# A decoder step on one core: unused products in front, a halved first transfer, and several moves in the order of work

## The chip, the cores and the metric

The kernel runs on one core of a Trainium2 chip. The metric is the device time of one execution in microseconds (us). A core has five engines with queues of their own: PE (matrix products and transposes, written to PSUM), DVE and ACT (vector and scalar work), POOL (here small copies, and the queue that issues some transfers) and SP (issues the other transfers). Sixteen DMA engines serve all queues.

## The reference, cut to what matters

One layer of a decoder works on 256 prompt rows and on 64 sample rows (8 sequences of 8 tokens, each with 1024 past positions in 8 pages). The rows are normed and go through one input projection:

```python
xn = rmsnorm(x, norm_mix)
proj = jnp.einsum('btd,dc->btc', xn, w_in)            # 1024 x 4888
# mixer A: compressed, selected and window attention, mixed by gates;
# the compression: hid = gelu(blocks @ w1), comp = hid @ w2
# mixer B: differential attention with its own keys and values
y_nsa  = jnp.einsum('btf,fd->btd', o_nsa.reshape(b, t, Q_NSA_W), w_br_nsa)
y_diff = jnp.einsum('btf,fd->btd', o_diff.reshape(b, t, V_DIFF_W), w_br_diff)
x = x + jnp.einsum('btd,de->bte', gate_nsa * y_nsa + gate_diff * y_diff, w_out)
h = rmsnorm(x, norm_ffn)
x = x + moe_ffn(h, ...)    # top 4 of 32 experts, each 1024 x 2048 and 1024 x 1024
```

`gate_nsa` and `gate_diff` are the sigmoids of the projection's last 2048 columns. Past keys and values come from paged caches by a page table.

## The kernel before

Everything is float32. Each engine's order is written out by hand, with semaphores between engines; a queue waits in order, so what stands behind a waiting instruction waits too. A product of float32 shows as two records of PE, and 512 columns are its widest.

**The head.** SP issues small constants, the three row tiles (`TILE_ORDER` is sample, prompt 0, prompt 1), then the chunks of `w_in`, 2 MB each, in slots of `wslot`. PE transposes each tile in two halves (`tp`, L2134). ACT evacuates the first half of a tile (L2386) and DVE the second (L2503), into `xnT`. ACT takes the squares for the norm (`square_of`, L2376), that of the first tile between two evacuations. Then `pe_projection` (L355 for prompt rows, L364 for sample rows) goes through chunks 0 to 5 in pairs; each product is 128 rows of `w_in` by 512 columns, 8 of them (`k`) for a row tile and a chunk.

**Transposes, gates, compression.** `qk_groups` are 15 groups of transposes. With the first eight PE does one of the 8 products of gate unit 0 each (`gate_products`, L2158); with the others four steps of the compression's first layer (`hidden`, L2170, 45 columns each). The twelve gate units fill PE between the stages of prompt attention: stage `s` is scores (L2212), gate units of `GATE_FIRST[s]`, transposed weights of the stage before, values. Scores of a stage wait for `e_ready`, the exponentials of the stage before (ACT, L2447).

**Turns.** Sample attention is done in 4 turns of two sequences. PE transposes pages of keys (`kd0` to `kd7` and `nk0` to `nk7`), selected keys (`sel`), window keys (`win`) and weights (`pd`, `ps`, `pw`, `pm`), in the order of `LOOP_GROUPS`; `l_tp` counts the groups. POOL's queue carries the pages for compression (`cmp_pages`, L469) and the differential values (`values_in`, L525); SP's carries the differential keys and the selected pages. DVE turns the compression pages of the next turn (L840) in its own order, ahead of evacuations of this turn; `dif_values` (L666) waits for the pages of `values_in`. In the last turn PE also does the branch products of the first output part (`branch_products(pe, 0, half)`, L1146), which wait for the semaphore `br`.

**Merge.** `sync_merge` is SP's queue from there: branch weights (`br_n`, `br_d`), the gates' stored values, `w_out`, small tensors and biases, and the experts' weights. PE's part is `pe_merge`: branch products, transposes of merged rows (`merged_t`, L1305, each after DVE's `m_done`), output products (`out_proj`, L1326), router logits, ranks, and the first rows picked for the experts (`first_pick`, L1365). The expert weights that take the place of `w_out` are issued after `z_full` is 5, that is after the last output product:

```python
            sp.wait_ge(z_full, 5)
            for h in range(2):
                down_weights(sp, 0, 0, h)
            down_weights(sp, 1, 1, 0)
            for c in range(4):
                sp.wait_ge(e_used, c + 1)
                gate_up_weights(sp, 1, c)
```

**Experts.** 32 experts, each with four 2 MB transfers (L1162) and two more (L1165, the last expert's in smaller pieces), stream through fixed places; a place is filled again when PE has used it (`e_used`).

## Time and profile before

| | us |
|---|---|
| median of 3 runs | 1439.93 |
| the runs | 1437.8 to 1440.52 |
| profiled execution, its own time | 1438.28 |
| its span in the profile | 1436.6 |
| PE busy | 1383.1 (96%) |
| DVE, ACT, POOL busy | 467.6, 285.6, 98.3 |

The span is the part from the first to the last instruction; the execution's time is 1.68 us more. PE is busy nearly throughout, but a busy PE may be one whose next record waits for data: the chain of work that ended last has 73% on PE and 18% on DMA.

### The profile page before, as it was taken

To read this page: it belongs to the slowest core of one execution; us is meant where nothing else is said; L and a number is where in the kernel's file an instruction comes from. 1 tells how busy PE (TensorE), PEld (TensorE's weight loads), DVE (VectorE), ACT (ScalarE), POOL (GpSimd) and SP (SyncE) were. 2 spreads that over 40 slices of the span, in tenths; PEclk is the share of its full clock that TensorE was granted. 3 is DMA by queue.
4 is the path that set the end of the run, shared out by engine and by line. 5 is a ranking of instruction groups with operands and counts; after the bars stand their busy time and mean duration, and the time that the engine had idled before them with its cause. 6 is when DMAs were issued, how large, how long until landed. Compare 5 with 4: busy or idle time off the path is not lost.

```text
span 1436.6 us, 19580 instructions
## 1 busy us (share of the span) xinstructions
PE 1383.1 (96%) x7350; PEld 610.6 (43%) x7350; DVE 467.6 (33%) x1022; ACT 285.6 (20%) x609; POOL 98.3 (7%) x217
## 2 busy tenths in 40 slices
PE   7999999999989999999999999999999999999987
PEld 3446555777764453333333333333333333333322
DVE  1113465555636352222133133121331331222314
ACT  2003344445542210110111100100111111010102
POOL 1000120624310000000000000000000000000000
PEclk9999999999999999999999999999999999999999
DMA  7334674899887599999999999999999999999996
GB/s 269 117 117 159 242 194 130 294 328 310 318 286 237 228 421 426 428 430 427 428 430 428 427 429 429 427 429 430 427 428 430 429 427 428 430 427 429 430 427 252
DMA packets 75468, 509.39 MB, mean 355 GB/s; under 512 B 19066, under 2 KB 25698, under 8 KB 46082
## 3 DMA queue, kind: packets, MB, share of 16 engines
q1 hardware_dynamic: 61378, 477.88, 81.7%
q0 software_dynamic: 13184, 27.82, 6.0%
q10 hardware_dynamic: 864, 3.15, 0.6%
q8 instruction: 25, 0.41, 0.1%
q14 instruction: 17, 0.14, 0.0%
HBM read 502.29 MB, written 10.62 MB: 357 GB/s over the span
## 4 chain that ended last, share of the span: by engine, by line
PE 73%; DMA 18%; DVE 3%; issue 3%; SPq 1%; ACT 1%; POOLq 0%; POOL 0%; DVEq 0%; ACTq 0%
PE PS L1464 25%; PE PS L1494 11%; DMA arena<-in_w_gate_up 10%; PE PS L1438 6%; PE PS L355 6%; DMA arena<-in_w_down 5%; PE PS L2158 4%; PE PS L1430 4%; PE PS L604 3%; PE PS L590 3%; PE PS L1326 2%; PE PS L364 1%; SPq L254 1%; PE PS L1481 1%; DMA arena<-in_cache_diff_k 1%
## 5 line engine op out<-in xcount | busy, mean ns | idle before, releaser
L1464 PE MATMUL PS<-arena 128*64 128x512 f32 x2048 | 456.1, 595 | 13.9 <-DMA arena<-in_w_gate_up 12.9
L1464 PEld LDWEIGHTS PS<-arena 128*64 128x64 f32 x2048 | 141.5, 137 | 294.9 <-issue 263.2
L1494 PE MATMUL PS<-arena 128*64 128x512 f32 x1024 | 226.9, 594 | 2.3 <-DMA arena<-in_w_down 2.2
L1920 DVE TENSOR_SCALAR arena<-PS 128x512 f32<-128x512 f32 x32 | 22.1, 692 | 450.9 <-PE PS L1473 449.9
L1494 PEld LDWEIGHTS PS<-arena 128*64 128x64 f32 x1024 | 71.7, 137 | 150.5 <-issue 144.3
L1438 PE MATMUL PS<-arena 128*128 128x512 f32 (+1 forms) x180 | 84.2, 608 | 0.0
L1430 PE MATMUL PS<-arena 128*128 128x512 f32 (+1 forms) x192 | 79.4, 618 | 4.5 <-ACT arena L1630 3.7
L355 PE MATMUL PS<-arena 128*128 128x512 f32 (+1 forms) x192 | 79.5, 576 | 1.9 <-DMA arena<-in_w_in 1.9
L1287 POOL COPY arena<-arena 96x64 bf16 (+1 forms) x34 | 8.1, 240 | 988.2 <-PE PS L1501 942.9
L1841 DVE TENSOR_TENSOR arena<-PS,arena 128x512 f32<-128x512 f32 x32 | 21.8, 688 | 162.1 <-PE PS L1446 161.2
L1615 ACT ACTIVATE arena<-arena 128x512 f32<-128x512 f32 x32 | 20.2, 631 | 268.1 <-DVE arena L1920 268.1
L1622 ACT ACTIVATE arena<-PS 128x512 f32<-128x512 f32 x32 | 19.1, 597 | 250.7 <-PE PS L1481 250.7
L604 PE MATMUL PS<-arena 128*128 128x252 f32 x256 | 68.1, 382 | 0.0
L590 PE MATMUL PS<-arena 128*128 128x128 f32 (+1 forms) x456 | 65.8, 277 | 2.3 <-DMA arena<-in_cache_diff_k 1.5
L1629 ACT ACTIVATE arena<-PS 64x512 f32<-64x512 f32 x31 | 18.3, 591 | 226.3 <-PE PS L1501 226.3
L590 PEld LDWEIGHTS PS<-arena 128*128 128x128 f32 (+1 forms) x456 | 53.1, 141 | 17.0 <-issue 5.8
L2158 PE MATMUL PS<-arena 128*128 128x512 f32 x128 | 59.6, 608 | 0.6 <-ACT arena L2395 0.6
L858 ACT ACTIVATE arena<-PS 128x512 f32<-128x512 f32 (+5 forms) x96 | 44.6, 492 | 61.4 <-PE PS L590 59.4
L355 PEld LDWEIGHTS PS<-arena 128*128 128x128 f32 x192 | 37.2, 195 | 43.7 <-issue 42.3
L1438 PEld LDWEIGHTS PS<-arena 128*128 128x128 f32 (+1 forms) x180 | 31.6, 188 | 46.3 <-issue 46.3
L604 PEld LDWEIGHTS PS<-arena 128*128 128x128 f32 x256 | 42.7, 190 | 4.6 <-issue 1.5
L1430 PEld LDWEIGHTS PS<-arena 128*128 128x128 f32 (+1 forms) x192 | 24.9, 171 | 43.9 <-issue 36.9
(289 smaller groups left out, 1280.9 us busy)
## 6 DMA issues: line engine op xcount, KB each, us to landing
arena<-in_w_gate_up SPq DMA_DIRECT2D x128, 2048.0 KB, 20.1
arena<-in_w_down SPq DMA_DIRECT2D x62, 2048.0 KB, 22.1
arena<-in_w_in SPq DMA_DIRECT2D x9, 2048.0 KB, 12.9
arena<-in_cache_diff_k SPq DMA_DIRECT2D x64, 256.0 KB, 6.0
arena<-in_cache_diff_v POOLq DMA_DIRECT2D x64, 256.0 KB, 5.0
arena<-in_cache_cmp_kv POOLq DMA_DIRECT2D x64, 128.0 KB, 3.9
arena<-in_cache_sel_kv SPq DMA_DIRECT2D x64, 128.0 KB, 6.9
arena<-in_w_out SPq DMA_DIRECT2D x1, 4096.0 KB, 14.2
```

The source lines that it names most:

```text
L355: last = nc.tensor.matmul(bank(proj_bank(q, 2 * s + t))[:, 0:w], xnT[:, k, 128 * t:128 * t + 128], chunk_at(j)[:, k, 0:w], start=(k == 0), ...
L590: last = nc.tensor.transpose(place[0:c, col:col + r], src, ident[0:r, 0:r])
L604: last = nc.tensor.matmul(hidden_at[c], w1[:, c, l, :], cmp_window(c, l), start=(l == 0), stop=(l == CB // 2 - 1))
L858: copy = lambda d, s: nc.scalar.activation(d, s, ACT.Copy)
L1326: last = nc.tensor.matmul(bank(Z_BANK[v])[p:p + r], mT[:, k, 128 * t:128 * t + r], w_out[:, k, 512 * nh:512 * nh + 512], start=(k == 0), s ...
L1430: last = nc.tensor.matmul(out, spread[:, 128 * t:128 * t + ROWS[t]], ypair[:, 512 * h:512 * h + 512], start=True, stop=True)
L1438: last = nc.tensor.matmul(bank(h), pick[0:ROWS[t], t], hn[t][0:ROWS[t], 512 * h:512 * h + 512], start=(t == 0), stop=(t == 2))
L1464: last = nc.tensor.matmul(bank(2 + role + 2 * u)[64 * h:64 * h + 64], hTm[:, k, BS * u:BS * u + BS], gu_w[:, k, D * role + 512 * h:D * rol ...
L1494: last = nc.tensor.matmul(bank(6 + u)[64 * h:64 * h + 64], aT[u][:, c % 4, 64 * (c // 4):64 * (c // 4) + 64], down_w[u][c // 4][:, c % 4, ...
L1841: st(V.tensor_tensor(hTm[:, :, BS * u:BS * u + BS], x, gffn.unsqueeze(2).to_broadcast([128, KD, BS]), ALU.mult), x_out)
L1920: st(V.tensor_scalar(g1, bank(2 + 2 * u), LIM, None, ALU.min), g1_ready)
L2158: last = nc.tensor.matmul(bank(7), xnT[:, k, 128 * t:128 * t + 128], chunk_at(j)[:, k], start=(k == 0), stop=(k == KD - 1))
```

## The change

Eight edits, in the order of the program:

- DVE sets 128x512 elements to 1 (`warm`), and PE does products on them that nobody reads: 512, 512 and 256 columns wide ahead of the first transposes, 256 after each of the first two tiles, 512 after the third. ACT takes the first tile's square after all evacuations.
- The first chunk of `w_in` comes in two transfers of half the rows (`k` 0 to 3, 4 to 7), and PE waits for the second after four products.
- The first three products of gate unit 1 are done with transpose groups 11, 12 and 13, among the compression's products, instead of after the first scores.
- POOL issues the compression pages of turn 1 before the differential values of turn 0. In the last turn the second sequence's values are issued after `kd7` instead of after `pd2`.
- The branch weights have two semaphores (`br_n`, `br_d`), and those of mixer A come as whole 128-partition transfers, one for each `k`, instead of half the partitions for two `k`.
- The first gate values (1 MB) are loaded with the other two, after the last scores.
- `branch(1)` goes ahead of PE's wait for the last evacuations of the turns.
- In the router's part, rows of tile 2 are picked where those of tile 0 were, and the other way about.

```diff
             past(pool, l_tp, NPAGE + group_at("kd0") + 1)
+            cmp_pages(pool, pages_of(POOL, 1, 0), 1, 0)
             values_in(pages[0], 0, 0, True)
             for n in (10, 11):
                 gates_stored(pool, n)
             pool.wait_ge(stored, n_stored)
-            cmp_pages(pool, pages_of(POOL, 1, 0), 1, 0)
             values_in(pages[1], 0, 1, True)
...
-                past(pool, l_tp, i * L_TP + (NPAGE + group_at("pd2", last) + 1))
+                past(pool, l_tp, i * L_TP + (NPAGE + group_at("kd7" if last else "pd2", last) + 1))
                 values_in(pages[1], i, 1)
...
                 if final:
-                    arrived(pe, "br")
+                    arrived(pe, "br_n")
                     branch_products(pe, 0, 0)
                 l_out_done(pe, i, group_at("pm", final), final)
                 nsa_values()
                 if final:
+                    arrived(pe, "br_d")
                     branch_products(pe, 0, 1).then_inc(br_full, 1)
...
             for c in range(2):
                 sp.wait_ge(l_hid, 2 * PAIRS_OF_SEQ - 1 + c)
-                for g in range(2):
-                    load(sp, "br", br_n[64 * g:64 * g + 64, 2 * c:2 * c + 2], w_nsa[g, :, 2 * c:2 * c + 2])
+                for k in (2 * c, 2 * c + 1):
+                    load(sp, "br_n", br_n[:, k], w_nsa[k])
                 for k in (c, c + 2):
-                    load(sp, "br", br_d[:, k], w_dif[:, k])
-                if c == 0:
-                    for n in (10, 11):
-                        gates_stored(sp, n)
-                    past(sp, l_tp, NPAGE + (PAIRS_OF_SEQ - 1) * L_TP + group_at("kd7", True) + 1)
-                    load(sp, "gates0", gsig[0:ROWS[0], 0], gate_pre[0:ROWS[0], 0:2 * D])
+                    load(sp, "br_d", br_d[:, k], w_dif[:, k])
+            for n in (10, 11):
+                gates_stored(sp, n)
             past(sp, l_sc, PAIRS_OF_SEQ * SCORES)
-            for t in (1, 2):
+            for t in range(3):
...
+            branch(1)
             l_out_done(pe, PAIRS_OF_SEQ - 1, len(LAST_GROUPS) - 1, True)
-            branch(1)
             branch(2)
...
-            for j in range(2):
-                load_chunk(j)
+            load(sp, "w_first", chunk_at(0)[:, 0:KD // 2], w_in[:, 0:KD // 2, 0:CHUNKS[0][1]])
+            sp.dma_start(chunk_at(0)[:, KD // 2:], w_in[:, KD // 2:, 0:CHUNKS[0][1]]).then_inc(w_arrived[0], 16)
+            load_chunk(1)
...
+            def unused_products(widths):
+                for w in widths:
+                    nc.tensor.matmul(bank(7)[:, 0:w], warm[:, 0:128], warm[:, 0:w], start=True, stop=True)
+
+            pe.wait_ge(warm_ready, 1)
+            unused_products((512, 512, 256))
             for k, t in enumerate(TILE_ORDER):
...
+                unused_products((256,) if k < 2 else (512,))
...
                     hidden(range(4 * (n - QK_HID), 4 * (n - QK_HID) + 4))
+                    if n in GATE_AMONG:
+                        gate_products(1, range(GATE_AMONG.index(n), GATE_AMONG.index(n) + 1))
...
-                    gate_products(g, range(KD if s < n - 1 else KD // 2))
+                    gate_products(g, range(0 if s else len(GATE_AMONG), KD if s < n - 1 else KD // 2))
...
+            V.memset(warm, 1.0).then_inc(warm_ready, 1)
```

`GATE_AMONG` is (11, 12, 13). `first_pick(0, ...)` and `first_pick(2)` change places in `pe_merge`, and `square_of` of the first tile moves behind the loop over tiles.

## Rows read from the trace of the kernel before

**Rows 1.** The page's 40 slices: GB/s that the DMA engines moved.
```profile
GB/s 269 117 117 159 242 194 130 294 328 310 318 286 237 228 421 426 428 430 427 428 430 428 427 429 429 427 429 430 427 428 430 429 427 428 430 427 429 430 427 252
```

**Rows 2.** The chain that ended last: start us, us, what.
```profile
3.50 10.29 DMA arena<-in_w_in
...
262.14 11.80 DMA arena<-in_cache_cmp_kv
...
466.58 0.46 PE PS L1305 x4
...
1418.27 3.65 PE PS L1494 x16
```

**Rows 3.** Waits of SP's queue: us in total, times, longest.
```profile
SPq L1165 <- PE PS L1326: 30.6, 1, 30.6
```

**Rows 4.** Timeline of PE at the last output products: start us, us, operation.
```profile
500.06 1.12 PE L1326 MATMUL PS<-arena 128*128 128x512 f32 x2
```

**Rows 5.** Timeline of the head; in brackets the idle time before, and its releaser.
```profile
5.49 1.31 PE L2134 MATMUL PS<-arena 8*128 8x8 f32 x9 [5.49 <-DMA arena<-in_x_sample]
...
10.11 1.94 PE L2134 MATMUL PS<-arena 128*128 128x128 f32 x8 [0.47 <-ACT arena L2386]
...
12.08 0.69 DVE L2503 TENSOR_TENSOR arena<-PS,arena 128x512 f32<-128x512 f32 x1 [1.72 <-PE PS L2134]
...
13.93 26.35 PE L355 MATMUL PS<-arena 128*128 128x512 f32 x55 [1.88 <-DMA arena<-in_w_in]
...
18.33 0.34 PEld L355 LDWEIGHTS PS<-arena 128*128 128x128 f32 x1 [0.52 <-issue]
...
19.52 0.19 PEld L355 LDWEIGHTS PS<-arena 128*128 128x128 f32 x1 [0.24 <-issue]
```

**Rows 6.** Windows: us; PE, PEld, DVE, ACT, POOL busy; PE clock, DMA share, GB/s.
```profile
10.00:25.00 15.00, 13.01 (x28) 6.42 (x29) 2.04 (x9) 5.80 (x13) 0.00 (x0) 1.00 1.06 388
...
136.00:138.00 2.00, 2.00 (x12) 1.92 (x13) 0.18 (x1) 0.45 (x2) 0.00 (x0) 0.50 0.03 8
```

**Rows 7.** Timeline of PE around the compression's products.
```profile
133.10 1.11 PE L2170 MATMUL PS<-arena 128*128 128x45 f32 x8
...
134.40 3.09 PE L2170 MATMUL PS<-arena 128*128 128x45 f32 x16
137.42 2.08 PE L2212 MATMUL PS<-arena 64*128 64x128 f32 x16
139.43 8.32 PE L2158 MATMUL PS<-arena 128*128 128x512 f32 x16
147.69 1.16 PE L2212 MATMUL PS<-arena 64*128 64x128 f32 x16
```

**Rows 8.** Timeline of ACT, the last of the first stage's exponentials.
```profile
143.84 0.37 ACT L2447 ACTIVATE arena<-PS,arena 128x128 f32<-128x128 f32 x1
```

**Rows 9.** Timeline of POOL's page transfers ahead of the first turn.
```profile
251.42 4.59 POOL L525 DMA_DIRECT2D arena<-in_cache_diff_v  x8 [9.85 <-PE PS L590]
258.05 4.67 POOL L469 DMA_DIRECT2D arena<-in_cache_cmp_kv  x8 [2.03 <-issue]
```

**Rows 10.** Timeline of PE: its idle places in the first and the last turn.
```profile
275.67 1.08 PE L734 MATMUL PS<-arena 128*64 128x512 f32 x4 [1.91 <-DVE arena L802]
...
412.08 1.96 PE L666 MATMUL PS<-arena 128*32 128x128 f32 x64 [0.87 <-DMA arena<-in_cache_diff_v]
...
418.70 3.70 PE L1146 MATMUL PS<-arena 128*128 128x512 f32 x8 [1.99 <-DMA arena<-in_w_br_diff]
...
429.47 14.00 PE L1146 MATMUL PS<-arena 128*128 128x512 f32 x32 [1.00 <-ACT arena L827]
```

**Rows 11.** Branch weights of mixer A: issue ns, starts, and us to landing.
```profile
L254 SPq DMA_DIRECT2D arena<-in_w_br_nsa x4: 609/627/712, 391.7 to 405.6; - x4
...
DMA to landing us min/median/max: 5.2/7.6/9.3
```

**Rows 12.** Timeline of DVE at the conversion of the biases.
```profile
449.00 1.76 DVE L1709 CAST arena<-arena 96x3072 bf16<-96x3072 f32 x1 [3.41 <-DMA arena<-in_b_down]
```

More of the change, by code:

```diff
@@ L190, in build @@
         gate_stage = [at(o1, 512) for o1 in (26112, 30720)]
+        warm = at(26112, 512)
         qraw, qrot, qdif = (at(26624 + 1536 * k, 3, 512) for k in range(3))
@@ L318, in build @@
         GATE_SPLIT = 6
+        GATE_AMONG = (11, 12, 13)
         GATE_SECOND = ((), (), (), (5,), (), (), (9,), (), ())
@@ L349, in pe_projection @@
                     w, slot = CHUNKS[j][1], CHUNK_SLOT[j]
-                    pe.wait_ge(w_arrived[slot], 16 * CHUNK_USE[j])
+                    if j == 0:
+                        arrived(pe, "w_first")
+                    else:
+                        pe.wait_ge(w_arrived[slot], 16 * CHUNK_USE[j])
                     for t in range(2):
@@ L354, in pe_projection @@
                         for k in range(KD):
+                            if j == 0 and t == 0 and k == KD // 2:
+                                pe.wait_ge(w_arrived[slot], 16)
                             last = nc.tensor.matmul(bank(proj_bank(q, 2 * s + t))[:, 0:w], xnT[:, k, 128 * t:128 * t + 128],
@@ L1404, in pe_merge @@
             logits(1, 0)
-            first_pick(0, range(4))
+            first_pick(2, range(4))
             x2_t(1, 1)
-            first_pick(0, range(4, KD))
+            first_pick(2, range(4, KD))
             logits(1, 1)
-            first_pick(2)
+            first_pick(0)
             pe.wait_ge(msk_ready, 2)
@@ L2387, in _ @@
                                             scale=gmix[:, m:m + 1]), tp_out[0] if m == 3 else None)
-                if k == 0:
-                    square_of(t)
-            for t in TILE_ORDER[1:]:
+            for t in TILE_ORDER:
                 square_of(t)
```

3 lines of the change are left out of this document (2 added, 1 removed).

## The prediction

> **What bounds the kernel now.** I read the page first: PE is busy for 96% of the span, and the chain puts 73% on it. That suggests that every us of PE counts alike. The slices of DMA traffic say otherwise [rows 1]: from slice 15 to the last but one it stands at 421 to 430 GB/s. Next I read when that stretch begins and what fills it. SP's queue has one wait of 30.6 us for PE's L1326 [rows 3]: the transfers that take the place of `w_out` stand behind the last output product, which ends at 500.06 + 1.12 = 501.2 us [rows 4]. Of the 32 x 6 = 192 transfers of 2 MB (2.097 million bytes) four of expert 0 and one of expert 1 are issued earlier; 187 are left, 392 MB, and at 428 GB/s they take 916 us: 501.2 + 916 = 1417, and the chain shows the last products starting at 1418.27 [rows 2]. So the kernel has two parts. Up to 501 us PE, with its waits, sets when the stream may start; after it the stream takes 917 us and an end of 18 us. Waits for weights after 501 us are not worth anything by themselves; what the last output product gains, the end gains, us for us. I therefore price each edit by what it does to 501.2.
>
> **The head.** PE's chain there: transposes of the third tile at 10.11, after waiting for ACT's evacuation; DVE's last evacuation ends at 12.08 + 0.69 = 12.77; the first chunk lands at 3.50 + 10.29 = 13.79; the projection starts at 13.93 after 1.88 us idle [rows 2, 5]. Its records are 0.34 + 0.52 = 0.86 us apart up to 19.1 us, and 0.19 + 0.24 = 0.43 us after it [rows 5]: 1.2 GHz, then 2.4 GHz (the window's clock says 1.00 in that stretch [rows 6]; the spacing is what I believe). Six records at the lower clock cost 6 x 0.43 = 2.6 us.
>
> The halved chunk: 1.05 MB less to wait for, at 388 GB/s [rows 6], is 2.7 us, so the first half lands near 11.1. The rest isn't late: four products at full clock take 8 x 0.43 = 3.4 us, and the second half lands near 13.8 plus about 0.1 for one more descriptor set. What is late next is the evacuation of the third tile. PE's unused products ahead of the transposes are 1280 columns, 2.5 x 2 records at 0.86 = 4.3 us from about 1.5 us on (the filling of `warm` is not in the trace; 0.69 us for a DVE operation of that size bounds it from above [rows 5], zero from below). They end near 5.8 us, against 5.49 for the first transposes [rows 5], and ACT's evacuation, which the next transposes wait for, hides that 0.3 us. The transposes themselves take 1.94 us for eight records at 1.2 GHz [rows 5], about 1.0 us at full clock. With ACT's square out of the way the third tile's start at about 9.5 instead of 10.1 and end at 10.5, DVE's evacuation ends at 11.3, and the last unused product (0.9 us) lies beside it. The projection starts near 11.4: 2.5 us gained. If its clock is up, 2.6 us more. The head gives 5.1 us; between 1.0 (12.9, only the transfer's wait gone) and 5.2. The projection behind it has no further wait of note, so this is carried on.
>
> The Trainium skill (TensorE: Matmul & The Clock Gate, Part 1) says that the throttled state is the default and that activity releases it; the spacing in rows 5 agrees. Part 4 of that page says that transposes do not engage the full clock as products do; by that rule PE, which has mostly transposes between 5.8 and 11.4 us, could be back at the lower clock, and the head would give 2.5 us.
>
> **Gate products among the compression's.** During the 45-column products the granted clock falls to 0.50, 1.2 GHz [rows 6]. The cost: 16 of them take 3.09 us where 8 took 1.11, so 0.9 more than twice that; the scores 2.08 against 1.16, 0.9; the 16 records of gate unit 1 8.32 against 16 x 0.43 = 6.9 plus 0.2, 1.2: 3.0 us [rows 5, 7]. The three moved products are 6 x 0.43 = 2.6 us of the same work at another place, wide products in the stretch that had none. I take it that the clock holds. But not all 3.0 us arrive. Those products hid ACT: scores of stage 1 wait for the exponentials of stage 0, which ended at 143.84 + 0.37 = 144.2, 4.7 us after the first scores ended (139.5) [rows 7, 8], while gate unit 1 covered 8.2 us. After the change the compression ends 2.6 - 0.9 = 1.7 us later and the first scores at 140.2. Left of gate unit 1 are 10 records, 4.3 us, up to 144.5; ACT's chain, which starts with the compression's end and has two table loads, ends 1.3 us later than before, 145.5. So scores of stage 1 start at 145.5 instead of 147.7: 2.1 us gained, PE idle for 1.0. Bounds: 0 (clock falls all the same) and 3.0.
>
> **Pages of turn 0 and 1.** In turn 0 PE waits 1.91 us for an evacuation by DVE [rows 10], which stood behind the turning of pages that landed at 262.14 + 11.80 = 273.9 [rows 2]. They are issued by POOL from 258.05, after 4.59 us of values and a reading of the page table [rows 9]. Put first, they are issued 4.6 us earlier (the reading stays ahead of them), land near 269, and the wait goes. The values take their place in the queue and end when the pages did, near 274; they are needed after L734, at 276.8, or 274.9 when the wait is gone. Gain 1.9 us, bounds 0 and 1.9, since the landing is close to the need. POOL's copies and its later transfers wait for other things and keep their times; keys for turn 1 are released by PE's own progress.
>
> **The last turn.** Values issued after `kd7` come earlier by the work of four groups (`kc`, `pd0` to `pd2`), and the 0.87 us wait for them goes [rows 10]; SP's selected pages share the DMA engines with them, bound 0. The wait of 1.99 us is for the last transfer of `br_d`, which is needed only behind 3.70 us of mixer A's branch products and the values after them [rows 10]. `br_n` is issued by 405.6 + 0.7 and takes at most 9.3 us: 415.6, and the need is at 418.70 - 1.99 = 416.7, 415.8 with the first wait gone [rows 10, 11]. The 1 MB of gate values that left the queue ahead of it (2.4 us at 428 GB/s) is spare. Gain 2.0, bounds 1.0 and 2.0. The shape of `br_n`'s transfers has no term of its own: same bytes, two issues as before.
>
> **The merge.** `branch(1)` fills the idle 1.00 us at 429.47 [rows 10]. Where does it go? The chain at 466.58 goes over DVE [rows 2]: transposes of the last merged rows wait for DVE, which waits for the biases, landed at 449.0 [rows 12], and they are issued by SP only after the last evacuation of the turns, which `branch(1)` doesn't move. PE gets there 1 us sooner and waits 1 us more. I count 0, at most 1.0. The three loads of gate values together are 2.6 MB, 6.1 us at 428 GB/s; they are issued before 412.08, and their first use is behind the last evacuation of the turns, that is after 429 [rows 10]. The exchanged picks are equal in number and length, beside the last output product, not ahead of it: 0, at most a few tenths.
>
> **The sum.** 5.1 + 2.1 + 1.9 + 0.9 + 2.0 + 0 = 12.0 us. Against the profiled execution: span 1436.6 - 12.0 = 1424.6, own time 1438.28 - 12.0 = 1426.3. The median of the runs, 1439.93, is 1.65 above that execution: 1427.9.
>
> **Rivals.**
> - *The clock is not held.* Either in the head (the unused products end 5.6 us before the projection, with transposes and little else between) or at the compression (the clock fell there with PE never idle [rows 6, 7]). The head's term is then 2.5: 1430.5; with both gone, 1432.6. For it: the low clock came with short records. Against: six more wide products stand in those stretches.
> - *The waits in the turns are DMA's and come back.* The DMA engines carry 286 to 328 GB/s in small rows from slice 8 to 12 [rows 1], and the three waits there are behind transfers. If pages are late whatever the order, 1.9 + 0.9 + 2.0 are lost: 1432.7. Against: `br_d` is plainly not needed yet when PE waits for it.
> - *Nothing arrives.* If something other than the last output product paced the stream, the time stays at 1439.9. The sum 501 + 916 speaks against it.
> - *Slower.* One mechanism: in turn 0 the first values are behind eight page transfers of POOL, and PE waits at L666. Each us later than 274.9 costs 1 us, against 12.0 us of gains: it decides if they land after 287, 25 us after their issue, where the pages took 11.80 [rows 2].
>
> **How the numbers follow.** The forecast, with each term within 2 us of its value, 0.58; the clock lost at one place or both 0.20; the waits that come back 0.13; nothing arrives 0.05; slower 0.04. The likeliest gives 1427.9, its own range is 1425 to 1430. For 8 in 10 I take in the clock rival with both places and most of the next: 1424.5 to 1433.5; the lower end is all upper bounds, 5.2 + 3.0 + 1.9 + 0.9 + 2.0 + 1.0 = 14.0, with a run's spread. Within 0.2% (2.9 us, about what a measurement of this kernel can tell from no change) lie the case in which nothing arrives and a part of it: 0.05. Faster 0.91, slower 0.04.
>
> **What would show it.** The first L355 record at 11.4 us, and all its weight loads 0.43 us apart; if some are 0.86 apart, the clock step fails. The clock at 1.00 through the compression, and an idle 1 us of PE ahead of the second scores. No idle ahead of L734 in turn 0, none of L666 or L1146 in the last turn. A new wait of about 1 us ahead of L1305. The last output product ending near 489.2, and GB/s at 428 from there on; if that stretch is not about 917 us, the frame of the prediction is wrong.

## The result and the profile after

| | before | after |
|---|---|---|
| median, us | 1440.22 (1437.8 to 1442.14) | 1470.39 (1466.88 to 1474.26, 4 runs) |
| profiled execution, its own time | 1438.28 | 1470.71 |
| its span | 1436.6 | 1469.0 |
| last output product ends | 501.18 | 529.78 |

The change makes the kernel slower: the ratio is 1.0197, 95% interval [1.0177, 1.0218]. The forecast was 1427.9, the range 1424.5 to 1433.5. One run of a later kernel (shape_back) took 1801 us at a granted clock of 0.75, a slow state that no other run shows, and stands in no median or ratio here.

The lines of the kernel after stand further down in the file: L1155 is L1146 of before, L1311 is L1305, L1332 is L1326, L674 is L666, L742 is L734.

**Where the time came from.** PE's longest waits between 255 and 500 us of the kernel after (who waited for whom: us in total, times, longest):

```profile
PE PS L1155 <- DMA arena<-in_w_br_nsa: 33.5, 1, 33.5
PE PS L674 <- DMA arena<-in_cache_diff_v: 3.5, 2, 3.2
PE PS L598 <- DMA arena<-in_cache_diff_k: 2.4, 3, 1.0
PE PS L1311 <- DVE arena L1703: 1.6, 1, 1.6
```

One wait is larger than the whole loss. It is for mixer A's branch weights, which before never held PE up by themselves [rows 10, 11]. PE's timeline there, and SP's queue (start us, us, operation; in brackets the idle time before and its releaser):

```profile
409.93 0.95 PE L598 MATMUL PS<-arena 128*128 128x128 f32 x7
444.41 6.36 PE L1155 MATMUL PS<-arena 128*128 128x512 f32 x8 [33.52 <-DMA arena<-in_w_br_nsa]
```

```profile
386.79 1.31 SPq L255 DMA_DIRECT2D arena<-in_w_br_nsa  x2
388.14 14.32 SPq L255 DMA_DIRECT2D arena<-in_w_br_diff  x2
402.51 12.90 SPq L255 DMA_DIRECT2D arena<-in_w_br_nsa  x2
415.45 10.85 SPq L255 DMA_DIRECT2D arena<-in_w_br_diff  x2
426.42 6.12 SPq L255 DMA_DIRECT2D arena<-gate_pre_scratch  x3
```

The windows of that stretch (us; PE, PEld, DVE, ACT, POOL busy; PE clock, DMA share, GB/s):

```profile
410.00:425.00 15.00, 0.88 (x7) 0.63 (x7) 1.45 (x9) 2.74 (x7) 0.00 (x0) 0.69 0.13 52
425.00:444.00 19.00, 0.00 (x0) 0.00 (x0) 0.00 (x0) 0.00 (x0) 0.00 (x0) 0.50 0.78 206
444.00:450.00 6.00, 5.59 (x7) 2.44 (x8) 0.00 (x0) 0.00 (x0) 0.00 (x0) 0.52 0.14 57
```

Look at the share of 0.13 and the 52 GB/s: that fits two of the sixteen DMA engines at 26 GB/s each (all sixteen move 428 [rows 1], 26.8 each), while the others stand idle. The four transfers hold 2.1 MB, and 2.1 MB at 52 GB/s are 40 us. From the first issue (386.79) to PE's start (444.41) it took 57.6 us; other transfers were under way for part of that time (206 GB/s from 425 to 444), so 40 us is the least and not the whole. Behind these transfers SP's queue itself stands: two issues of `br_d` took 1.08 us before and take 14.32 and 10.85 us now. The same place of the queue before:

```profile
404.99 1.27 SPq L254 DMA_DIRECT2D arena<-in_w_br_nsa  x2
406.30 1.08 SPq L254 DMA_DIRECT2D arena<-in_w_br_diff  x2
```

PE gets to the branch products at 409.93 + 0.95 = 410.88, before it was 418.70 - 1.99 = 416.71 [rows 10]: the rest of the change had brought 5.8 us. The new wait is 33.52 - 1.99 = 31.5 us more than the old one, and the eight records after it take 6.36 instead of 3.70 us [rows 10], because PE's clock fell to 0.50 while it stood: 2.7 more. 31.5 + 2.7 - 5.8 = 28.4; the last output product ends 28.6 us later.

**What answers to the other rows of before.** The head and the compression (PE's timeline), then turn 0:

```profile
1.62 4.61 PE L2147 MATMUL PS<-arena 128*128 128x512 f32 x6 [1.62 <-DVE arena L2513]
...
10.05 1.07 PE L2141 MATMUL PS<-arena 128*128 128x128 f32 x8 [0.45 <-ACT arena L2403]
...
11.95 1.52 PE L363 MATMUL PS<-arena 128*128 128x512 f32 x3
...
132.64 2.00 PE L2185 MATMUL PS<-arena 128*128 128x45 f32 x16
134.57 1.16 PE L2229 MATMUL PS<-arena 64*128 64x128 f32 x16
135.66 4.56 PE L2173 MATMUL PS<-arena 128*128 128x512 f32 x10
140.90 1.16 PE L2229 MATMUL PS<-arena 64*128 64x128 f32 x16 [0.68 <-ACT arena L2462]
...
268.22 1.96 PE L674 MATMUL PS<-arena 128*32 128x128 f32 x64
...
274.29 1.95 PE L674 MATMUL PS<-arena 128*32 128x128 f32 x64 [3.17 <-DMA arena<-in_cache_diff_v]
```

The projection starts at 11.95 (13.93 before [rows 2, 5]) and every record of it is 0.43 us apart; the second scores come at 140.90 (147.69 [rows 7]). Both gains are there. In turn 0 the wait of 1.91 us for DVE ahead of L742 is gone [rows 10], and one of 3.17 us for the second sequence's values stands in its place.

The stream of expert weights takes 1450.70 - 529.78 = 920.9 us, before 917.1 (1418.27 - 501.18); the last 3.8 us of the loss are there.

### The profile page after: what moved, and what is told of

The parts are those of the page before. It is cut to its first block, busy times and chain, and to the rows that moved or that the text cites. A ratio compares the mean times of both kernels' runs of the same rounds, so it can differ in the third digit from the quotient of the medians.

```text
span 1469.0 us, 19606 instructions
## 1 busy us (share of the span) xinstructions
PE 1386.6 (94%) x7362; PEld 608.9 (41%) x7362; DVE 467.6 (32%) x1023; ACT 285.4 (19%) x609; POOL 98.2 (7%) x217
## 4 chain that ended last, share of the span: by engine, by line
PE 69%; DMA 21%; issue 3%; SPq 3%; DVE 2%; ACT 2%; POOLq 0%; POOL 0%; DVEq 0%; ACTq 0%
PE PS L1470 24%; DMA arena<-in_w_gate_up 11%; PE PS L1500 10%; PE PS L1444 6%; PE PS L363 5%; DMA arena<-in_w_down 4%; PE PS L2173 4%; PE PS L1436 3%; DMA arena<-in_w_br_nsa 3%; PE PS L598 2%; SPq L255 2%; PE PS L1332 2%; PE PS L612 2%; PE PS L372 1%; DMA arena<-in_cache_diff_v 1%
## 5 line engine op out<-in xcount | busy, mean ns | idle before, releaser
L1444 PE MATMUL PS<-arena 128*128 128x512 f32 (+1 forms) x180 | 84.2, 608 | 0.0
L1436 PE MATMUL PS<-arena 128*128 128x512 f32 (+1 forms) x192 | 79.4, 617 | 4.5 <-ACT arena L1636 3.7
L363 PE MATMUL PS<-arena 128*128 128x512 f32 (+1 forms) x192 | 77.0, 561 | 0.0
L1155 PE MATMUL PS<-arena 128*128 128x512 f32 (+1 forms) x96 | 38.1, 626 | 33.5 <-DMA arena<-in_w_br_nsa 33.5
L598 PEld LDWEIGHTS PS<-arena 128*128 128x128 f32 (+1 forms) x456 | 53.0, 141 | 17.2 <-issue 6.1
L1444 PEld LDWEIGHTS PS<-arena 128*128 128x128 f32 (+1 forms) x180 | 31.6, 188 | 46.3 <-issue 46.3
```

What stands on the lines that cost most here:

```text
L363: last = nc.tensor.matmul(bank(proj_bank(q, 2 * s + t))[:, 0:w], xnT[:, k, 128 * t:128 * t + 128], chunk_at(j)[:, k, 0:w], start=(k == 0), ...
L598: last = nc.tensor.transpose(place[0:c, col:col + r], src, ident[0:r, 0:r])
L1155: last = nc.tensor.matmul(bank(BRANCH_BANK[v][half])[p:p + r], src[:, k, 128 * t:128 * t + r], w[:, k, 512 * nh:512 * nh + 512], start=(k ...
L1436: last = nc.tensor.matmul(out, spread[:, 128 * t:128 * t + ROWS[t]], ypair[:, 512 * h:512 * h + 512], start=True, stop=True)
L1444: last = nc.tensor.matmul(bank(h), pick[0:ROWS[t], t], hn[t][0:ROWS[t], 512 * h:512 * h + 512], start=(t == 0), stop=(t == 2))
```

## The experiments

All times in one table. "Cast" is when DVE starts to convert the biases in the merge [rows 12]; "last" is the end of the last output product. Ratios are to the kernel before on the same chips.

| kernel | median us | ratio, interval | cast | last |
|---|---|---|---|---|
| before | 1440 to 1443 | 1 | 449.00 | 501.18 |
| after | 1470.39 | 1.0197 [1.0177, 1.0218] | 477.60 | 529.78 |
| shape_alone | 1480.17 | 1.0266 [1.0242, 1.0290] | 486.45 | 538.62 |
| shape_back | 1437.48 | 0.9959 [0.9943, 0.9976] | 445.33 | 497.50 |
| pages_alone | 1443.34 | 1.0007 [0.9994, 1.0019] | 455.64 | 507.80 |
| pages_back | 1433.88 | 0.9945 [0.9928, 0.9963] | 444.98 | 497.16 |
| among_back | 1437.60 | 0.9972 [0.9957, 0.9987] | 449.35 | 501.52 |
| unused_back | 1435.11 | 0.9942 [0.9922, 0.9962] | 442.94 | 496.81 |
| late_gates | 1434.66 | 0.9935 [0.9917, 0.9954] | 443.81 | 495.98 |
| kd7_back | 1434.06 | 0.9935 [0.9915, 0.9955] | 444.25 | 497.10 |
| one_wait | 1436.57 | 0.9956 [0.9934, 0.9977] | 442.98 | 495.16 |
| bias_alone | 1441.14 | 0.9997 [0.9981, 1.0013] | 444.96 | 500.36 |
| bias_first | 1430.45 | 0.9920 [0.9897, 0.9943] | 435.46 | 487.72 |

Cast and last come from one profile each, and a kernel's executions differ by some us (bias_first: 1425.3 to 1433.3). The experiments ran on four chips, on which the kernel before had medians of 1442.4 to 1443.4, so across groups of experiments the ratios say more than the medians. The profile of the kernel before is of an execution of 1438.28, some 4 us below those medians: differences between its "last" and another kernel's come out smaller than those between the medians.

Four edits were never undone or made alone: the halved first chunk with the moved square, `branch(1)` ahead of the wait, the later first gate values, and the exchanged picks.

### The shape of the branch weights' transfers

shape_back undoes this edit alone in the changed kernel; shape_alone makes it alone in the kernel before:

```diff
-            w_nsa = io["w_br_nsa"][0].rearrange("(g r d) n -> r g d n", g=2, r=4)
+            w_nsa = io["w_br_nsa"][0].rearrange("(g r d) n -> g d r n", g=2, r=4)
...
-                for k in (2 * c, 2 * c + 1):
-                    load(sp, "br_n", br_n[:, k], w_nsa[k])
+                for g in range(2):
+                    load(sp, "br_n", br_n[64 * g:64 * g + 64, 2 * c:2 * c + 2], w_nsa[g, :, 2 * c:2 * c + 2])
```

> The changed kernel with one edit undone: mixer A's branch weights come again as two transfers per half over 64 partitions each; everything else of the change stays. Theory (the shape of these transfers alone is the loss): the 33.5 us wait ahead of the branch products goes; their landing is 5 to 9 us again, PE starts them at about 411, the last output product ends near 492 (501.2 before), and the time is 1429 to 1433 us, 7 to 11 below the kernel before. Rival 1 (the loss is in the order of SP's queue or in the split semaphores, not in the shape): most of the wait stays and the time is above 1455. Rival 2 (the stream of expert weights is itself slower by about 4 us after the change, as in the changed kernel's profile, 920.9 against 917.1): the wait goes but the time is 1433 to 1437.

> The kernel before with only the new shape of mixer A's branch weights (whole partitions, one transfer per k whose source has an outermost dimension of 2); order of queues and semaphores as before. Theory: the transfers move at about 52 GB/s, 2.1 MB in 40 us, and PE waits some 30 us more: 1465 to 1475 us. Rival (it takes the shape and the split semaphores or the new queue order together): below 1450 us.

Measured: shape_back is faster than the kernel before by 0.4%, 5.9 us, and PE does not wait for these weights in its profile. shape_alone is slower by 38 us, 5 us more than its theory's upper end; its profile has the wait (there both mixers' weights have one semaphore, so it is put down to `br_d`, which came last):

```profile
454.19 5.48 PE L1146 MATMUL PS<-arena 128*128 128x512 f32 x8 [31.00 <-DMA arena<-in_w_br_diff]
```

By the ratios the shape costs 0.0238 of 1440 us, 34 us, in the changed kernel, and 38 us on the kernel before. It needs no other part of the change. But shape_back came out at 1437.48 and not at the 1429 to 1433 of its theory: something else of the change falls short. The stream, which rival 2 named, took 920.0 us in this profile, 2.9 more than before. More stands in turn 0:

```profile
269.75 1.95 PE L674 MATMUL PS<-arena 128*32 128x128 f32 x64 [1.64 <-DMA arena<-in_cache_diff_v]
277.74 1.67 PE L674 MATMUL PS<-arena 128*32 128x128 f32 x25 [5.09 <-DMA arena<-in_cache_diff_v]
```

**What about the shape is slow?** With r in front, the source of one transfer has the dimensions g (2), d (64), n. In the old shape the loop had taken g out, and the source was d (64), r (2), n. Two kernels keep everything of the change (whole partitions, one transfer for each k, three dimensions, rows of 1024 floats, that is 4 KB, and not 2 as the expectation below has it) and give the outermost dimension another size. The weight rows then lie in another order, so mixer A's branch product is computed with permuted weights. Its values are other values, they reach the router, and both kernels did 34 expert passes instead of 32 (136 transfers of `w_gate_up` instead of 128, in all 25.2 MB more from HBM, 58.8 us at 428 GB/s): their whole times cannot be set beside the others, which was not foreseen, but everything up to the last output product can.

```diff
-            w_nsa = io["w_br_nsa"][0].rearrange("(g r d) n -> r g d n", g=2, r=4)
+            w_nsa = io["w_br_nsa"][0].rearrange("(r d g) n -> r g d n", r=4, g=16)
```

> The changed kernel, but the source rows are grouped so that the outermost dimension of each source pattern is 16 instead of 2 (it still has three dimensions, fills 128 partitions and moves the same bytes in rows of 2 KB). The rows then sit on other partitions, so mixer A's branch product is computed with permuted weight rows; its work is the same. Theory (the outermost dimension sets how many DMA engines share a transfer): 16 engines, landing 5 to 9 us, no long wait, 1429 to 1433 us. Rival (a three-dimensional source or a transfer of whole partitions as such is slow): like the changed kernel, near 1470 us.

> As the one with 16, but with an outermost dimension of 4: the dose. Mixer A's branch product again takes permuted weight rows. Theory: four DMA engines, about 104 GB/s, 2.1 MB in 20 us from 402.5 or somewhat earlier; PE waits until 422 to 426 instead of 444.4, 11 to 15 us, and the time is 1443 to 1450 us. Rival (slow as such): near 1470 us; rival (only 2 is slow): like the kernel with 16.

Measured: with 16 PE starts the branch products without a wait for the weights, `br_n` lands in 9.0 us (median), and the last output product ends at 494.45:

```profile
411.33 3.60 PE L1155 MATMUL PS<-arena 128*128 128x512 f32 x8
```

With 4 (PE's timeline, and the windows while the last of them are under way):

```profile
427.13 5.89 PE L1155 MATMUL PS<-arena 128*128 128x512 f32 x8 [16.56 <-DMA arena<-in_w_br_nsa]
```

```profile
420.00:422.00 2.00, 0.00 (x0) 0.00 (x0) 0.00 (x0) 0.00 (x0) 0.00 (x0) 0.50 1.01 156
422.00:424.00 2.00, 0.00 (x0) 0.00 (x0) 0.00 (x0) 0.00 (x0) 0.00 (x0) 0.50 0.50 82
424.00:426.50 2.50, 0.00 (x0) 0.00 (x0) 0.00 (x0) 0.00 (x0) 0.00 (x0) 0.50 0.26 102
```

The wait is half of the 33.52 us with 2, and the tail runs at a share of 0.26, four engines of sixteen, and 102 GB/s, twice the 52. With the 58.8 us taken off, an estimate, the times of the one run of each are 1432.6 and 1453.2 us, the second 3 us over its theory, which had the wait at 11 to 15 us and had forgotten the clock behind it (5.89 us for the eight records). Both rivals, a three-dimensional source or whole partitions as such, fall. The outermost dimension of the source sets how many engines share a transfer here: two with 2 and four with 4. With 16 the limit is gone; that it is sixteen engines then, no window shows by itself. The Trainium skill states such a rule (DMA: Bandwidth & Descriptors, section "Why a DMA increments its semaphore by 16 and not by 1"): the number of engines is the largest up to 16 that divides the slowest dimension larger than one of both patterns. The traces agree, with 0.13 of the engines at 2 and 0.26 at 4.

### The order of POOL's transfers in turn 0

```diff
-            cmp_pages(pool, pages_of(POOL, 1, 0), 1, 0)
             values_in(pages[0], 0, 0, True)
             for n in (10, 11):
                 gates_stored(pool, n)
             pool.wait_ge(stored, n_stored)
+            cmp_pages(pool, pages_of(POOL, 1, 0), 1, 0)
             values_in(pages[1], 0, 1, True)
```

pages_back is shape_back with this undo as well; pages_alone is the kernel before with the new order alone.

> The kernel with the branch weights' old shape, and with POOL's old order in turn 0 too (values of pair 0 first, then the wait for the stores, then turn 1's pages, then the second values). Theory (the new order makes the values of turn 0 late, 1.64 + 5.09 us of waits in the profile of the kernel without this undo; the old order cost PE one wait of 1.91): these two waits go, the old one of about 1.9 may come back, the last output product ends 4 to 6 us earlier, at 492 to 494, and the time is 3 to 6 us below the same kernel with the new order, 1432 to 1435 us beside 1438. Rival (PE reaches turn 0 6.8 us earlier and the DMA engines are full there, so the waits come whatever the order): the sum of waits in turn 0 stays at 5 us or more and the time is within 1.5 us of 1438.

> The kernel before with only POOL's new order in turn 0 (turn 1's pages first, then all values). Theory (the values are late by themselves): PE waits 2 to 7 us ahead of the value products of turn 0 instead of 1.91 us for DVE; 1443 to 1447 us beside 1442 for the kernel before. What the prediction said: 1.9 us gained, 1440. Rival (the order costs only where PE comes early): within 1 us of the kernel before.

Measured: in pages_back the two waits for values go and the old one for DVE comes back; in pages_alone the waits for values appear:

```profile
PE PS L1155 <- DMA arena<-in_w_br_nsa: 2.8, 1, 2.8
PE PS L742 <- DVE arena L811: 2.0, 1, 2.0
```

```profile
276.62 1.95 PE L666 MATMUL PS<-arena 128*32 128x128 f32 x64 [0.39 <-DMA arena<-in_cache_diff_v]
283.61 1.72 PE L666 MATMUL PS<-arena 128*32 128x128 f32 x28 [4.08 <-DMA arena<-in_cache_diff_v]
```

The waits move as the theory says. The times say it more weakly: pages_back is 3.6 us below shape_back in the median, within the expected 3 to 6, but by the ratios it is 2.0 us, and the two intervals overlap; pages_alone (one us above the kernel before in the median) cannot be told from no change, although its profiled execution, the slowest of its ten, is 6.6 us behind the kernel before at the last output product. The prediction's gain of 1.9 is contradicted by the waits for values in turn 0 of five profiles with the new order (after, shape_back, pages_alone, outer16, outer4: 3.2, 6.7, 4.5, 4.2 and 4.0 us). Why pages_back's branch weights now came 2.8 us late, though in shape_back they were in time, was open at this point (the section on the last turn takes it up); its last output product was only 0.3 us earlier than shape_back's, not 4 to 6.

### The two edits for the clock

among_back takes the three gate products out of the compression again, unused_back takes out the unused products; both on pages_back:

```diff
-                    if n in GATE_AMONG:
-                        gate_products(1, range(GATE_AMONG.index(n), GATE_AMONG.index(n) + 1))
```

```diff
-            unused_products((512, 512, 256))
...
-                unused_products((256,) if k < 2 else (512,))
```

> Old shape, old order of turn 0, and no gate products among the compression's (all sixteen of gate unit 1 follow the first scores again). Theory (the clock falls to 0.50 there without them): clock 0.50 at 132 to 140 us, PE reaches turn 0 2.3 us later; if turn 0 passes that on, the time is 2.3 us above the same kernel with them. Rival (turn 0 waits for DMA either way and takes the gain back): the waits in turn 0 are 1 to 2 us shorter, and the time is less than 1 us above.

> Old shape, old order of turn 0, the first chunk in halves as changed, but no unused products. Theory (they raise the clock and cost nothing, because PE waits there): the projection starts at about 11.4 to 12 us all the same, its first six weight loads are 0.86 us apart, and PE is 2.5 us later from there on; the time is 1.5 to 2.5 us higher. Rival (the clock rises by the transposes and the first products of the projection themselves at the same moment): less than 0.5 us. Rival (the unused products hold up the transposes): the projection starts earlier than 11.95 without them.

Measured for among_back: the clock falls (windows), and PE begins turn 0 at 239.57, against 235.08 in pages_back. Of these 4.5 us 0.7 are older than the compression, so the edit is worth 3.8 there. That is more than the 2.3 between before and after, because the clock fell earlier: the window from 130 to 135 has 0.54 here, where the kernel before had 1.00 up to 134 us, and gate unit 1 took 9.17 us instead of 8.32 [rows 7]. The time is 3.7 us higher by the medians, 3.9 by the ratios (the intervals overlap a little, [0.9957, 0.9987] and [0.9928, 0.9963]).

```profile
130.00:135.00 5.00, 5.00 (x28) 4.72 (x29) 1.32 (x7) 1.84 (x4) 0.86 (x3) 0.54 0.05 16
135.00:140.00 5.00, 5.00 (x20) 2.82 (x19) 3.11 (x7) 4.46 (x13) 0.69 (x1) 0.50 0.95 313
```

Measured for unused_back: the projection starts at 12.68, since the transposes ahead of it are at the lower clock again (eight records in 1.94 us), and its weight loads are 0.34 + 0.52 = 0.86 us apart up to 17.4:

```profile
13.67 0.34 PEld L363 LDWEIGHTS PS<-arena 128*128 128x128 f32 x1 [0.52 <-issue]
14.52 0.34 PEld L363 LDWEIGHTS PS<-arena 128*128 128x128 f32 x1 [0.52 <-issue]
```

The projection's prompt rows end at 105.94 instead of 103.08: the unused products are worth 2.9 us of PE there, and the halved chunk with the moved square the other 1.4 (107.32 before). Yet the whole time is the same within the intervals (0.9942 against 0.9945). PE was 2.8 us later at the start of turn 0 (237.92) and came 2.6 us earlier to the branch products (410.66 against 413.22). A gain ahead of the turns does not pass through them whole. No gain of the unused products in the whole time is shown, and this is the first sign of a second pace-maker.

### The last turn

On pages_back again, one edit each: late_gates holds SP's loads of gate values back (they went out at 406.46 instead of 403.77, not at 409 as meant); kd7_back lets the last turn's second values wait for `pd2` again; one_wait makes PE wait for all branch weights at once.

```diff
+            past(sp, l_tp, NPAGE + (PAIRS_OF_SEQ - 1) * L_TP + group_at("ps1", True) + 1)
             for t in range(3):
                 load(sp, f"gates{t}", ...)
```

```diff
-                past(pool, l_tp, i * L_TP + (NPAGE + group_at("kd7" if last else "pd2", last) + 1))
+                past(pool, l_tp, i * L_TP + (NPAGE + group_at("pd2", last) + 1))
```

```diff
                     arrived(pe, "br_n")
+                    arrived(pe, "br_d")
                     branch_products(pe, 0, 0)
```

> Old shape, old order of turn 0, and SP's three loads of gate values held back until PE's group ps1 of the last turn (about 409 us instead of 403.8). Theory (in the profile without this edit PE waits 2.78 us for br_n, because 2.6 MB of gate values and br_d are under way beside it, and its next eight records take 5.29 us instead of 3.70): br_n lands before 410.5, both costs go, the last output product ends 3 to 4.4 us earlier, at 493 to 494, and the time is 3 to 4 us below 1433.9. Rival (br_n's landing is set by the values and selected pages of the turn, or differs from run to run): the wait stays, and the time is within 1.5 us of 1433.9.

> Old shape, old order of turn 0, and POOL's second values of the last turn wait for group pd2 again instead of kd7. What the prediction said (0.9 us for this edit): PE waits 0.5 to 1 us for these values at about 406 us again, and the time is up to 1 us above 1433.9. Rival (earlier values delay br_n by sharing the DMA engines): the wait of 2.78 us for br_n shrinks or goes, and the time is 1 to 3 us below.

> Old shape, old order of turn 0, and PE waits for both mixers' branch weights ahead of the first branch product, as the kernel before does (the semaphores stay apart, PE waits for both). What the prediction said (2.0 us for the split wait): PE waits for br_d, which in the profile without this edit lands at about 415.5 to 416.5, so 2.5 to 3.3 us later than br_n, and the time is 2 to 4 us above 1433.9. Rival (a later wait takes the gain: L1311 behind DVE's merge, or the stream): less than 1 us above.

Measured, PE's first branch products in pages_back, then in late_gates, kd7_back and one_wait:

```profile
413.22 5.29 PE L1155 MATMUL PS<-arena 128*128 128x512 f32 x8 [2.78 <-DMA arena<-in_w_br_nsa]
```

```profile
410.91 6.33 PE L1155 MATMUL PS<-arena 128*128 128x512 f32 x8 [3.25 <-DMA arena<-in_w_br_nsa]
```

```profile
409.80 3.70 PE L1155 MATMUL PS<-arena 128*128 128x512 f32 x8
```

```profile
411.55 5.14 PE L1155 MATMUL PS<-arena 128*128 128x512 f32 x8 [2.63 <-DMA arena<-in_w_br_diff]
```

The theory of late_gates falls. PE came at 410.91 - 3.25 = 407.66, 1.2 us after the first of the gate values was issued, and `br_n`, the last of it issued by 398.3, was not there; its median landing took 12.3 us, against 11.6 in pages_back. In kd7_back the wait is gone, as its rival said, and `br_n` lands in 7.6 us. The other profiles side with that: the median landing of `br_n` is 9.0 to 12.3 us in the seven kernels that issue the second values after `kd7` and have an outermost dimension of 16 or more (shape_back, pages_back, among_back, unused_back, late_gates, one_wait, outer16), and 7.5 to 7.9 us in the five that issue them after `pd2` (before, pages_alone, bias_alone, kd7_back, bias_first). So the earlier values delay `br_n`. Whether PE waits for it is another matter: shape_back, unused_back and outer16 had no such wait. In exchange PE waits 0.33 us for the values in kd7_back (expected 0.5 to 1). one_wait's median is 2.7 us above pages_back, 1.6 by the ratios, less than the intervals can tell from zero.

What matters more is that none of the three is clearly faster than pages_back (by the ratios 1.4 us at most, inside the intervals), though in kd7_back PE begins the branch products 3.4 us earlier. Its merge shows where that went:

```profile
452.18 1.08 PE L1311 MATMUL PS<-arena 128*128 128x128 f32 x4 [3.69 <-DVE arena L1709]
```

```profile
444.25 1.76 DVE L1715 CAST arena<-arena 96x3072 bf16<-96x3072 f32 x1 [8.83 <-DMA arena<-in_b_down]
...
451.35 0.68 DVE L1709 COPY arena<-PS 128x512 f32<-128x512 f32 x1
```

DVE waits 8.8 us for the biases, then converts them, and PE's transposes stand behind that. In the table, last minus cast is 52.16 to 52.18 us in all kernels down to one_wait, the one before among them (501.18 - 449.00), but for kd7_back and unused_back with 52.9 and 53.9, where PE waits for DVE (3.69 us; 1.51 and 1.74) and its clock is below 1 behind the wait (0.50 from 452 to 456; 0.83 from 460 to 470). So the biases' landing looks like what paces the merge. SP issues them behind the router's weights, whose one issue holds the queue:

```profile
415.78 0.39 SPq L255 DMA_DIRECT2D arena<-in_w_out  x1
420.58 0.82 SPq L255 DMA_DIRECT2D arena<-in_norm_ffn  x2
421.44 9.45 SPq L255 DMA_DIRECT2D arena<-in_w_router  x1
430.93 2.90 SPq L255 DMA_DIRECT2D arena<-in_b_router  x1
```

The kernel before has the same distance, but PE without a wait at that place:

```profile
466.06 0.98 PE L1305 MATMUL PS<-arena 64*128 64x64 f32 x8
```

In pages_back `w_out` is issued 5.0 us later (420.79), the router's weights take 5.36 us, and their issue ends at 431.8, against 430.9 here. Of the 5 us by which PE's turns end earlier, less than one reaches the biases.

### The biases first

bias_first is kd7_back, bias_alone the kernel before, each with this move:

```diff
+            for s in range(3):
+                load(sp, "bias", b32[32 * s:32 * s + 32, 0:2 * D], io["b_gate_up"][0])
+                load(sp, "bias", b32[32 * s:32 * s + 32, 2 * D:3 * D], io["b_down"][0])
             load(sp, "late", gffn, io["norm_ffn"].rearrange("a (p k) -> p (a k)", k=KD))
...
-            for s in range(3):
-                load(sp, "bias", b32[32 * s:32 * s + 32, 0:2 * D], io["b_gate_up"][0])
-                load(sp, "bias", b32[32 * s:32 * s + 32, 2 * D:3 * D], io["b_down"][0])
```

> The kernel with the old shape, the old order of turn 0 and the old place of the last turn's second values, and SP's six loads of biases moved ahead of the router's and norms' loads that follow the turns. In that kernel's profile without this edit DVE's cast of the biases starts at 444.25, although PE began the branch products at 409.80, and the last output product ends 52.85 us after the cast (52.18 in the kernel before). Theory (the biases' landing paces the merge, and a slow issue of the router's weights, 9.45 us in SP's queue, makes them late): the cast starts 6 to 12 us earlier, PE's idle of 3.69 us ahead of L1311 goes, the last output product ends at 492 to 493.5 instead of 497.10, and the time is 3.5 to 5 us below 1434.1. Rival (the biases' cast is only a neighbour of what paces the merge, or the loads put behind them come late in its place): less than 1 us.

> The kernel before with only the same move of the biases' loads. Theory (in the kernel before PE reaches the last transposes of the merge just as DVE is done, without an idle above 0.3 us): the cast starts some 6 us earlier, at about 443, but the last output product ends at 500.5 to 501.2, and the time is within 1 us of the kernel before: the biases bind only once PE comes earlier. Rival (they pace the kernel before too): 2 us or more below.

Measured, the cast of bias_first, then the start of its branch products and its last output product:

```profile
435.46 1.76 DVE L1715 CAST arena<-arena 96x3072 bf16<-96x3072 f32 x1 [3.05 <-DMA arena<-in_b_down]
```

```profile
406.88 3.60 PE L1155 MATMUL PS<-arena 128*128 128x512 f32 x8
...
486.60 1.12 PE L1332 MATMUL PS<-arena 128*128 128x512 f32 x2
```

The cast starts 8.8 us earlier and no wait ahead of L1311 is left. From the start of the branch products to the end of the last output product it is 487.72 - 406.88 = 80.8 us, where kd7_back took 497.10 - 409.80 = 87.3: in this pair of profiles the merge gave 6.5 us. The median is 1430.45, 3.6 us below kd7_back; ratio 0.9920 [0.9897, 0.9943], 11.5 us (8.2 to 14.9) faster than the kernel before. Against kd7_back the intervals still overlap; that the wait has gone is shown by the profile, the size of the gain is not closely known. Part of this profile's 487.72 is luck in the turns (its execution, 1425.3, is the fastest of six, and turn 0's wait for DVE, 0.2 to 2.6 us in the others with the old order, did not come). The same move on the kernel before changes nothing (0.9997 [0.9981, 1.0013]), although its cast is 4.0 us earlier: there PE arrives just in time. Both go as the theory said, but for the last output product of bias_first, which ended 4 us earlier than the theory had it. bias_first has the lowest median of this study.

## Why the prediction was wrong, point by point

**The step that failed** is the sentence "The shape of `br_n`'s transfers has no term of its own: same bytes, two issues as before." It counted bytes and issues, not the engines that share a transfer, and so the term for the last turn took over `br_n`'s old landing, "at most 9.3 us", for transfers that no longer had the old pattern. The runs put 34 us (shape_back against after) to 38 us (shape_alone) in its place. No rival had it: the one on the slower side was the values of turn 0. Nor would the forecast have held without this step: with the old shape back the rest of the change brought 5.9 us, half of the 12.0.

**The head.** Predicted 5.1, measured 4.49 (102.83 against 107.32). Three other profiles with the old head (pages_alone, bias_alone, shape_alone) end there at 106.1 to 106.6, as their weight loads come to 0.43 us apart 1.4 to 2.2 us earlier; so 3.2 to 4.5 is the fair figure. The clock held, transposes included: eight records in 1.06 us. The halves landed at 11.1 and 13.9, as forecast; the start came at 11.95 instead of 11.4, because the third tile's transposes started at 10.05 instead of 9.5, behind ACT.

**The compression.** Predicted 2.1, measured 2.3, and 3.8 against among_back; the idle place of PE was 0.68 instead of 1.0 us. The mechanism held. How much it gives depends on when the clock falls without it.

**The pages of turn 0.** Predicted +1.9, measured a loss of 1.5 in the profile after (from the start of turn 0 to the second value products 274.29 - 234.83 = 39.5 us, before 279.63 - 241.62 = 38.0), and worse waits in others. The slower rival had the right mechanism (values behind eight page transfers) at the wrong transfers: it priced the first eight values. Late are the second eight, issued until 260.5 and landed at 274.2, when PE wanted them at 271.1. The term also took over landing times of the old order. POOL now issues 24 transfers in one go, and what the engines move meanwhile changes (windows before, then after):

```profile
250.00:260.00 10.00, 10.00 (x86) 7.63 (x84) 2.77 (x4) 4.30 (x7) 6.22 (x12) 1.00 0.98 386
```

```profile
250.00:260.00 10.00, 10.00 (x81) 7.18 (x80) 3.52 (x9) 4.46 (x10) 9.16 (x18) 1.00 1.03 277
```

Both are full, at 386 and 277 GB/s. The slow stretch is not new: before, it comes later, with the pages (241 GB/s from 265 to 270 at a share of 1.09). It has moved ahead of the values. In the kernel before the first eight values, ahead of it, landed in 6.1 us (median); now all sixteen are behind it and take 11.1 us, the longest 14.2. The kernel before already had its second eight behind the pages, 10.4 us and at most 12.0, but PE wanted them later, at 279.6. The prediction had named the low rates of this stretch [rows 1] under a rival with a chance of 0.13, and left them out of this term.

**The last turn.** The wait of 0.87 us is gone, and that of 1.99 for `br_d` too, the latter no wonder behind 33.52 us for `br_n`. Once the shape is undone, a wait of 2.6 to 3.3 us for branch weights came in four of the six kernels that keep `kd7` (pages_back, among_back, late_gates, one_wait). Predicted 0.9 + 2.0. The lower bound of 0 for the earlier values was wrong: it reckoned with the selected pages beside them, and the cost fell on `br_n`, which took 9.0 to 12.3 us instead of 7.5 to 7.9. What the two edits are worth is not settled closer than that a gain or a loss of 3 us is possible.

**The merge.** Zero for `branch(1)` fits: the idle 1.00 us of before is gone, and a wait of 1.55 us ahead of L1311 is new. No kernel undoes this edit alone. But the reason given for it, that the last merged rows wait for the biases whatever PE does, was not carried to its end. It caps every gain ahead of it, not that of `branch(1)` alone. With the two faulty edits undone 8 us of the 12 arrived (pages_back, 0.9945 of 1442.4); with `kd7` back and the biases moved too, 11.5. That the total then comes near 12.0 is luck: it lacks the new shape and two edits that the prediction priced at 1.9 and 0.9, and contains one that the prediction did not have.

**The frame.** That the end follows the last output product held: from there to the last weights' use it took 917.0 to 918.5 us in seven kernels with 32 passes, and 919.2 to 920.9 in the six others. Those six are the ones whose windows between 500 and 600 us show PE's clock below 1 for a moment (after: 0.83 from 560 to 570). That this moment is what the stream loses there is likely and not shown. Whether the change makes it likelier is open; the kernel before with one edit shows it as well.

## What to carry to other kernels

Before a transfer's pattern is called the same bytes, read the size of its outermost dimension on both sides. Outermost dimensions of 16 and 64 were free of the loss here, 2 and 4 were not. When a wait is long, look for a DMA share near 2/16 or 4/16. An edit that brings PE earlier is worth only what the next fixed arrival allows: take the distance between each late landing and the end across profiles, and where it is constant, suspect that landing. A constant distance is not proof: in the kernel before it is there too, and moving the biases alone gave nothing. Ahead of a stretch in which the DMA engines are full, an order change is a trade between two waits and cannot be priced by the old order's landing time.

## What the runs showed of the hardware

- Transfers whose source's outermost dimension is 2 moved 52 GB/s at a share of 0.13 (after), and with 4 102 GB/s at 0.26 (outer4), that is about 26 for each engine; with 16 they landed in 9.0 us, median, and at most 13.6 (outer16).
- The issuing queue is held behind such transfers as well: the two issues of 512 KB that followed a pair of them took 14.3 and 10.9 us with 2 (after), and 1.0 and 5.7 us with 4 (outer4), where before it was 1.1.
- PE's granted clock was 0.50 while it stood still from 425 to 444 us (after), and the work behind a wait can pay for it: eight records of the branch products took 6.36 us behind a wait of 33.52, 6.33 behind 3.25 (late_gates), 5.29 behind 2.78 (pages_back), 5.14 behind 2.63 (one_wait), 5.40 behind 2.12 (pages_alone), and 3.70 behind 1.99 us [rows 10].
- The clock held at 1.00 through PE's transposes in the head behind unused products (eight records in 1.06 us instead of 1.94), and through the compression with six wide records among its short ones.
- A load of 2 MB in two halves landed at 11.1 and 13.9 us, where the whole had landed at 13.8.
- Values issued earlier on POOL's queue slowed transfers on SP's: `br_n` took 9.0 to 12.3 us behind the earlier values, 7.5 to 7.9 without (median of four).
- A single issue of the router's weights (128 KB) occupied SP's queue for 4.4 to 9.9 us (shape_alone, bias_first). What sets the time was not tested; the distance from the issue of `w_out` was 5.7 us both at 5.3 (before) and at 9.5 us (kd7_back).
